# The index score stage of a two-block attention kernel holds no top-k selection rounds; all of them are pulled in the mixer's steps

## What is computed

```python
logits = jnp.einsum('bqhd,bkd->bqhk', iqb, ik).astype(jnp.float32) * (IDX_DIM ** -0.5)
score = jnp.einsum('bqhk,bqh->bqk', jax.nn.relu(logits), iwb)
score = jnp.where(kpos[None, None, :] <= qpos[None, :, None], score, NEG)
_, idx = lax.top_k(score, topk)      # topk = 256
```

## Time and profile before

| what | value |
|---|---|
| median of 3 runs | 3756.22 us (3756.02 to 3757.26) |
| the profiled execution: its own time | 3758.67 us |
| its span, first to last instruction | 3756.9 us |
| granted TensorE clock, mean | 0.982 of full |
| busy in the span: TensorE, VectorE, ScalarE, GpSimd | 95%, 46%, 21%, 2% |
| index stage, about 1737 to 1904 us | 24 steps |
| mixer's branch 0, about 1904 to 2054 us | 16 steps |
| branches 1 and 2, about 2054 to 2410 us | 32 steps |

### The profile page before, as it was taken

The page is one execution under the profiler, slowest core; times in us unless marked ns, Lnnn a source line. Parts: engine busy times, 40 slices in busy tenths (PEclk is TensorE's granted clock), DMA queues, the critical chain, the costliest instruction groups (busy, mean ns, idle before and its releaser), DMA issues.

```text
span 3756.9 us, 30976 instructions
## 1 busy us (share of the span) xinstructions
PE 3555.0 (95%) x12602; PEld 1866.6 (50%) x12602; DVE 1730.4 (46%) x2802; ACT 807.2 (21%) x1670; POOL 70.2 (2%) x91
## 2 busy tenths in 40 slices
PE   7999999999989999999769899999999999999998
PEld 3556555565456444544445555574444444444443
DVE  2166281023156350243988889753033655253433
ACT  4244012012244111122224332331121000000001
POOL 0000000020000000100000000000000000000000
PEclk9999999999999999999989999999999999999999
DMA  5100221230000102101000000121101111111111
GB/s 214 44 1 12 72 84 65 93 112 31 25 6 12 33 31 98 48 31 51 12 34 34 23 29 29 57 74 45 39 6 39 39 40 42 48 45 36 42 37 64
DMA packets 53353, 176.27 MB, mean 47 GB/s; under 512 B 5679, under 2 KB 9007, under 8 KB 52539
## 3 DMA queue, kind: packets, MB, share of 16 engines
q1 hardware_dynamic: 48344, 158.40, 11.9%
q10 hardware_dynamic: 4868, 15.91, 1.2%
HBM read 170.04 MB, written 11.32 MB: 48 GB/s over the span
## 4 chain that ended last, share of the span: by engine, by line
PE 83%; DVE 13%; ACT 2%; issue 1%; SPq 1%; DMA 1%; POOL 0%; DVEq 0%; ACTq 0%; POOLq 0%
PE ps L476 41%; PE ps L1047 13%; PE ps L817 4%; PE ps L567 4%; DVE sb L1944 3%; PE ps L702 3%; DVE sb L1942 3%; PE ps L590 2%; PE ps L716 2%; PE ps L579 2%; PE ps L828 1%; PE ps L895 1%; DVE sb L1998 1%; PE ps L906 1%; DVE sb L1724 1%; PE ps L995 1%
## 5 line engine op out<-in xcount | busy, mean ns | idle before, releaser
L476 PE MATMUL ps<-sb 128*128 128x512 f32 (+1 forms) x3856 | 1565.5, 567 | 12.8 <-ACT sb L1366 6.8
L476 PEld LDWEIGHTS ps<-sb 128*128 128x128 f32 x3856 | 733.1, 191 | 837.8 <-issue 817.7
L1106 ACT ACTIVATE sb<-ps 128x512 f32<-128x512 f32 (+9 forms) x650 | 326.0, 515 | 1696.8 <-PE ps L476 541.3
L1047 PE MATMUL ps<-sb 128*128 128x512 f32 x1232 | 531.4, 594 | 2.9 <-DVE sb L2197 2.9
L1047 PEld LDWEIGHTS ps<-sb 128*128 128x128 f32 x1232 | 234.6, 191 | 299.1 <-issue 293.6
L817 PE MATMUL ps<-sb 128*128 128x512 f32 x512 | 238.1, 614 | 0.0
L1148 ACT ACTIVATE sb<-sb 128x512 f32<-128x512 f32 x128 | 76.2, 614 | 478.9 <-DVE sb L1903 157.5
L1942 DVE MAX8 sb<-sb 128x8 f32<-128x384 f32 (+5 forms) x192 | 171.5, 893 | 4.8
L1944 DVE MATCH_REPLACE8 sb<-sb 128x384 f32<-128x384 f32 (+5 forms) x192 | 168.1, 876 | 0.0
L567 PE MATMUL ps<-sb 96*128 96x512 f32 (+1 forms) x400 | 158.2, 531 | 7.5 <-ACT sb L1280 4.0
L1840 DVE SCALAR_TENSOR_TENSOR sb<-sb 128x1310 f32<-128x1310 f32 (+1 forms) x120 | 161.6, 1438 | 0.0
(11 more groups left out here) (175 smaller groups left out, 2946.8 us busy)
## 6 DMA issues: line engine op xcount, KB each, us to landing
sb<-in_w_in SPq DMA_DIRECT2D x73, 512.0 KB, 3.3
sb<-in_w_ada SPq DMA_DIRECT2D x48, 512.0 KB, 4.4
sb<-in_w_up SPq DMA_DIRECT2D x44, 512.0 KB, 3.3
sb<-in_dft SPq DMA_DIRECT2D x32, 512.0 KB, 3.2
sb<-in_w_down SPq DMA_DIRECT2D x24, 384.0 KB, 3.0
sb<-in_w_out SPq DMA_DIRECT2D x16, 512.0 KB, 3.3
sb<-in_w_mkv SPq DMA_DIRECT2D x16, 512.0 KB, 3.2
rows_dram<-vec_dram ACTq DMA_DIRECT2D x1, 6906.0 KB
```

Of the source, the lines that this page charges most:

```text
L476: ins = mm(ps[:, 0:tn], w[:, k, :], src(k, t0, tn), start=(k == 0), stop=(k == nk - 1))
L1047: ins = mm(ps[:, 0:512], stationary(k), moving(k), start=(first and k == 0), stop=(k == 3), skip_group_check=not first)
L1106: return act(out, in_, func, scale=scale)
```

## The change

The two lines of VectorE's index loop that pull rounds after each weighting are gone. `first` is worked out from `columns[0]`, so the shares of the first 16 steps follow from it; nothing else in the text of the kernel differs.

```diff
                 ins.then_inc(*e.step(("weighted", n)))
                 e.wait_ge(*at(("weighted", n)))
-                for _ in range(min(t - 2, 2)):
-                    columns[0] += next(rounds)
```

## The result

The changed kernel takes 3799.11 us (median of 4 runs, 3796.65 to 3802.76) against 3756.74 for the kernel before (4 runs): a ratio of 1.0112, 95% interval 1.0094 to 1.0130. It is slower by 42.4 us; 42.5 were forecast, with a range of 3786 to 3822 us. The profiled execution of the changed kernel took 3802.76 us, 3801.0 of span.

A forecast was written before the change was run, and what follows sets the result against it. VectorE was taken to bound the index stage and, but for 19.2 us of waits, branch 0. The terms -47.1 + 89.6 = +42.5 us take the median from 3756.22 to 3798.7 us, range 3786 to 3822.

The forecast's parts named there:

- Step 1: Price on VectorE of the 72 rounds and two closing instructions moved from index stage to branch 0: 103.8 us.
- Step 2: Index stage: without rounds TensorE bounds it, and VectorE starts the mixer's first scored tile 47.1 us earlier.
- Step 3: Branch 0: 150.0 + 103.8 - 19.2 of waits + 5 at `turned` = 239.6 us, 89.6 more.
- Step 4: Branches 1 and 2 and the rest: same instructions, 0 taken; slower clock up to 3, TensorE's lead up to 5 back.
- A: Rival: TensorE's slow clock becomes a bound in branch 0, 28 us of waits plus 3 at transposes, 3830; chance 0.10.
- B: Rival: VectorE's waits in branch 0 do not all go, up to 14 of 19.2 us stay, 3813; chance 0.08.
- C: Rival: rounds find idle time in all three branches and the kernel is not slower, -17.0 us, 3739; chance 0.02.
- D: Rival: downstream, TensorE's lead and a smaller wait at `turned` give some back, about 3788; chance 0.06.

The follow-up runs named there:

- drop72: Changed kernel with the 72 moved rounds left out, selection incomplete, shares starting at 0.25 again; 3715.46 us, ratio 0.9881 to the kernel before.
- one_round: Kernel before with one round after each weighting from t = 3 on, instead of up to two; 3756.36 us, ratio 0.9993.
- after_warm: Changed kernel in which TensorE repeats the attention scores of each odd step of branch 0; 3798.37 us, ratio 1.0109 to the kernel before.
- spread: Changed kernel with shares 0.255 and 0.545 in place of 0.45 and 0.65, rounds over all three branches; 3780.29 us, ratio 1.0059 to the kernel before.
- spread_warm: The spread kernel with TensorE repeating scores in each odd step of branches 0 and 1; 3763.43 us, ratio 1.0013 to the kernel before.
- one_round_paced: The one_round kernel with shares 0.345 and 0.59 in place of 0.45 and 0.65; 3743.37 us, ratio 0.9958 to the kernel before.

## Why the prediction was right, by its steps

**Step 1, the price of the rounds: 103.8 us forecast.** Branch 0 less its waits is 235.56 - 1.3 = 234.3 us after and 150.04 - 19.2 = 130.8 before, so the moved rounds cost 103.4 us there. A round takes as long in the mixer as in the index stage: its MAX8 of 512 columns takes 0.69 us on the mean in either.

**Step 2, the index stage: -47.1 forecast, -45.5 measured.** The bound after it is TensorE, as said. The step was mis-sized in one term: the values that fill t = 6 and 7 take 1839.59 - 1835.93 = 3.66 us, not 3.45. Eight times 0.2 us are the 1.6 that were missing. The 3.45 was taken from branch 0, and rows 5 had the right one at hand: 1887.36 - 1883.71 = 3.65, in the stage itself. Why the same 16 matmuls leave 0.2 us more in front of scores I did not test.

**Step 3, branch 0: +89.6 forecast, +85.5 measured.** The waits for the root and the exponentials went completely, as forecast. The remaining waits were 1.3 us, not 5: those at `turned` came to 0.8 in three steps, so the value should have been taken near the lower bound of 0 to 8. Drop72 confirms the two terms separately, since it has one without the other.

**Step 4, the rest: 0 forecast, +1.2 and +1.7 us measured** in branches 1 and 2, inside the 3 that were allowed. The traces put both down to TensorE's slow clock, at the entry to branch 1 as this step says, and once more in branch 2. The first filler of branch 1 and one filler of branch 2, first in the kernel before, then in the changed one; the last line is the division behind the first of them:

```profile
2054.28 3.60 PE L817 MATMUL ps<-sb 128*128 128x512 f32 x8
...
2262.08 3.62 PE L828 MATMUL ps<-sb 128*128 128x256 f32 x16
```

```profile
2099.67 5.68 PE L817 MATMUL ps<-sb 128*128 128x512 f32 x8
...
2307.66 5.31 PE L828 MATMUL ps<-sb 128*128 128x256 f32 x16
```

```profile
2108.30 0.41 DVE L2042 TENSOR_SCALAR sb<-ps,sb 128x128 f32<-128x128 f32 x1 [3.21 <-ACT sb L1526]
```

Over the first 10.3 us of branch 1 the granted clock was 0.72, against 1.00 before, and this division waited 3.21 us where it had waited 1.11; three steps on, a shorter wait gives most of the loss back, and 1.2 stay. The 1.7 of branch 2 are the 5.31 - 3.62 of its filler: the scores behind it come that much later, and VectorE waits 4.12 us for them instead of 2.44. The same filler takes 5.31 us in one_round and 5.30 in after_warm, where branch 2 takes 203.9 us too, and 3.62 in drop72, where it takes 202.2. TensorE had waited 3.26 us ahead of it before as well as after, so that wait alone does not decide it; what does was not tested, and no run here changes this one burst by itself.

**The sum** is closer than its terms, and that is luck: the misses of +1.6, -4.1 and +2.9 cancel to 0.4, and the runs of the changed kernel alone lie up to 6 us apart.

**The rivals.** A is the one to learn from. Its mechanism was there (clock 0.82 in branch 0 and bursts of 9.69 us), its price in branch 0 was zero, and the reason is the comparison that the prediction made: 11.0 us of chain against 14.5 of VectorE's own work. The bursts recovered on the way, too, as assumed: 9.69 us is well short of the 14.06 of a burst at 1.2 GHz throughout. Spread, where that margin is gone, pays for the slow bursts, and spread_warm gets 17.6 us back. The rule of the Trainium skill ("TensorE: Matmul & The Clock Gate", section "HAM oscillation"), that a loop whose matmul burst is shorter than the wait after it starts each burst cold, agrees with the first steps of the branch. The matmuls of step 2 last 4.6 us, 9.99 of idle follow, and the next two fillers take 8.77 us instead of 7.03; those of step 1 last 10.8 us, 3.53 of idle follow, and the next filler takes 3.60 us, as at full clock. So it was not every step that paid with TensorE's time, as the prediction read the rule: all eight pairs of fillers were slow, but five of the seven single ones in steps 2 to 14 were not. B fell: no wait at the division is left. C's mechanism, measured by spread, gives 19 us of the 42 back (3799 to 3780) and does not turn the sign, because the waits do not all take rounds: 33.8 us of 67.7 stayed. D had one part right, the smaller wait at `turned`; but nothing was given back behind branch 0, where the changed kernel lost 2.9 us.

**What follows for the change.** The rounds of the index stage were not wrong there, they were too many: up to two per weighting hold up TensorE, one fits under its step nearly free (122.4 against 119.6 us). And here the early start was worth less than the deferred work cost, because all of that work went to one branch that VectorE already bounds.

## What to carry to other kernels

When work is moved along the queue of an engine, look at the idle time that it meets: here its duration did not change (103.4 us for 103.8), only the idle did. Write down that engine's waits in the stretch it leaves and in the stretch it enters: here 58.1 us of new waits on one side (18.4 to 76.5) against 17.9 removed on the other (19.2 to 1.3), 40.2 of the 42. And deal such filler work out by what the other engine has to do in each step, not evenly: that alone, with the same number of rounds in every branch, gave 26 us of the before kernel's time.

## What the runs showed that I had not expected

- More work on TensorE made a kernel faster: repeated scores in its gaps raised the granted clock from 0.88 to 0.99 and took 10.6 us off branch 0 (spread against spread_warm), 17 us off the whole.
- Adding rounds to a step does not lower its waits smoothly. Branch 0 waits 19.2 us with 4.6 us of rounds in a mean step (before), 22.8 with 5.4 (one_round_paced), 13.3 with 6.6 (spread), 10.3 with 7.9 (one_round) and 1.3 with 11.1 (after). The rounds are an estimate: the branch less its waits and 57 us of other work (a third of the 172 that spread's expectation has for three branches), over 16. The clock falls along: 0.95 before, 0.91 in one_round_paced, 0.88 in spread, 0.84 in one_round, 0.82 after. That longer gaps of TensorE bring slow bursts, which eat the first of the added cover, fits these numbers, but only spread was tested for it.
- The same code ahead of the index stage ends at different times: its first matmul (L802) starts at 1736.93 us in the kernel before, 1741.37 after, and 1737.95, 1734.79, 1738.43 and 1733.30 in drop72, spread, one_round and one_round_paced. Differences of up to 8 us between single profiled executions were there before any edited code ran.
